# Reordering the first block of a two-block transformer kernel, and dispatching experts inside the turn

## What is computed

```
x: (1, 256, 1024), all float32
first_block, 2 layers l:
  u, q, k, v, gate = rms_norm(x, norm1[l]) @ w_in[l]      # 1024 | 1536 | 1536 | 1536 | 2048 columns
  pooled = multi-window average pooling of u, minus u, through w_pool[l], times pool_scale[l]
  attn   = 12 heads of attention over 256 tokens, with a relative bias table
  m      = gate_a * (pooled @ w_a[l]) + gate_b * (attn @ w_b[l]);  x = x + m @ w_o[l]
  x      = x + (gelu(conv(a)) * b) @ w_down[l]   with a, b = rms_norm(x, norm2[l]) @ w_up[l]
second_block (one layer, with 256 context tokens and a modulation vector silu(c) @ w_ada + b_ada):
  rms_norm(norm_f(x)), modulated; projections; two recurrent mixers and a windowed attention; w_out
  hierarchical mixture of 32 experts (4 groups of 8, the best 2 of the best group per token),
  each expert: (silu(h @ w_gate) * (h @ w_up)) @ w_down
```

## Time and profile before

| | us |
|---|---|
| median of 3 runs | 1995.33 (1994.34 to 1996.38) |
| the profiled execution | 1991.78 |
| its span | 1990.0 |
| TensorE busy, weight loads busy | 1699.0, 1311.2 |
| VectorE, ScalarE, GpSimd busy | 871.2, 596.9, 115.0 |

### The profile page before, as it was taken

One profiled execution on the slowest core, in us unless ns is written; L12 is line 12 of the kernel. 1 busy time (PEld: TensorE's weight loads), 2 busy tenths in 40 slices (PEclk: granted clock), 3 DMA queues, 4 the chain that ended last, 5 costly groups with the idle time before them and its releaser, 6 DMA issues.

```text
span 1990.0 us, 32401 instructions
## 1 busy us (share of the span) xinstructions
PE 1699.0 (85%) x14363; PEld 1311.2 (66%) x14363; DVE 871.2 (44%) x1202; ACT 596.9 (30%) x761; POOL 115.0 (6%) x103
## 2 busy tenths in 40 slices
PE   6999899999899989999989998696987866556665
PEld 6999898998699989899847554385865322112221
DVE  3445566664443556666423744775724111001111
ACT  4344445543334444555321021324213010000000
POOL 0500000000050000000022410000000000000000
PEclk9999999999899999999999998798998998889888
DMA  8651365754675136596434110000069999999998
GB/s 281 230 180 64 127 228 215 271 207 155 234 259 190 64 128 228 213 334 221 148 59 140 43 43 11 1 3 2 3 243 351 373 409 410 410 410 409 410 410 326
DMA packets 154958, 419.94 MB, mean 211 GB/s; under 512 B 14050, under 2 KB 20893, under 8 KB 151762
## 3 DMA queue, kind: packets, MB, share of 16 engines
q1 hardware_dynamic: 154402, 417.87, 56.7%
q10 hardware_dynamic: 432, 0.22, 0.0%
HBM read 416.18 MB, written 1.89 MB: 210 GB/s over the span
## 4 chain that ended last, share of the span: by engine, by line
PE 63%; DMA 19%; DVE 10%; ACT 5%; issue 3%; DVEq 0%; SPq 0%; ACTq 0%
PE bank L1182 29%; DMA R<-w_exp_down 8%; DMA R<-w_exp_up 7%; PE ps_s L1292 3%; PE ps_t L1292 3%; PE bank L1370 3%; PE ps_s L1345 3%; PE bank L1345 2%; ACT w_high L1782 2%; DVE w_low L2187 2%; PE bank L1737 2%; DMA wring<-w_up 2%; PE bank L1722 1%; PE ps_t L1352 1%; DMA wring<-w_in 1%
## 5 line engine op out<-in xcount | busy, mean ns | idle before, releaser
L2187 DVE TENSOR_TENSOR w_low<-wring,w_high 128x2048 fp32r<-128x2048 f32 (+1 forms) x128 | 289.1, 2258 | 329.0 <-ACT w_high L1782 328.4
L1782 ACT ACTIVATE w_high<-wring 128x2048 fp32r<-128x2048 f32 (+1 forms) x128 | 238.2, 1861 | 355.8 <-PE bank L1182 300.0
L1182 PE MATMUL bank<-x_high,w_high 128*128 128x256 f32 x1600 | 325.9, 285 | 18.3 <-DVEq L2215 11.5
L1182 PE MATMUL bank<-x_low,w_high 128*128 128x256 f32 x1600 | 321.5, 283 | 0.0
L1182 PE MATMUL bank<-x_high,w_low 128*128 128x256 f32 x1600 | 319.7, 281 | 0.0
L1182 PEld LDWEIGHTS bank<-x_high,w_high 128*128 128x128 f32 x1600 | 247.4, 191 | 26.0 <-DVEq L2215 12.6
L1182 PEld LDWEIGHTS bank<-x_high,w_low 128*128 128x128 f32 x1600 | 247.8, 190 | 0.0
L1182 PEld LDWEIGHTS bank<-x_low,w_high 128*128 128x128 f32 x1600 | 246.8, 190 | 0.0
L1737 PE MATMUL bank<-R 128*32 128x512 f32 x640 | 94.8, 727 | 63.7 <-DMA R<-w_exp_up 47.9
L1737 PEld LDWEIGHTS bank<-R 128*32 128x32 f32 x640 | 19.9, 124 | 128.6 <-DMA R<-w_exp_up 68.5
L2842 DVE TENSOR_TENSOR R<-bank,R 128x512 f32<-128x512 f32 x8 | 5.5, 693 | 202.3 <-PE bank L1737 202.3
(11 more groups left out here) (584 smaller groups left out, 2688.8 us busy)
## 6 DMA issues: line engine op xcount, KB each, us to landing
wring<-w_in SPq DMA_DIRECT2D x37, 2048.0 KB, 8.0
R<-w_exp_up SPq DMA_DIRECT2D x24, 2048.0 KB, 23.8
R<-w_exp_down SPq DMA_DIRECT2D x24, 2048.0 KB, 23.8
wring<-w_up SPq DMA_DIRECT2D x22, 2048.0 KB, 9.0
R<-w_exp_gate SPq DMA_DIRECT2D x16, 2048.0 KB, 23.4
wring<-w_exp_gate SPq DMA_DIRECT2D x16, 2048.0 KB, 23.7
wring<-w_ada SPq DMA_DIRECT2D x12, 2048.0 KB, 10.8
wring<-w_down SPq DMA_DIRECT2D x10, 2048.0 KB, 7.8
```

What stands on the lines that cost most here:

```text
L1182: mm = pe.matmul(b[:, i * S:(i + 1) * S], left, right, start=k == 0 and m == 0 and i == 0, stop=k == last and m == 2, skip_group_check=True)
L1782: a.activation(high_of(l, job), half_block(l, job, wring), ACT.Copy).then_inc(w_high_ready, 1)
L2187: v.tensor_tensor(half_block(l, job, w_low), half_block(l, job, wring), high_of(l, job).bitcast(F32), ALU.subtract).then_inc(w_low_ready, 1)
```

## The change

- *Start*: the gain row is loaded to one partition by ScalarE's queue, ahead of `ident`; TensorE spreads it by two matmuls with a row of ones into `ps_t`; VectorE multiplies h by it before the norm is known. 1/rms becomes a diagonal matrix (`by_rms`), and layer 0's four `x1` jobs are matmuls with it in place of transposes. The first block comes in two DMAs of four row tiles; high and low parts of its first job are made in halves, the first between `x1` 1 and 2. An operation of the square root function stands ahead of the squares.
- *Order of blocks*: `ada` 4 ahead of `down` 5; `u` 0 of layer 1 ahead of `ada` 5.
- *Gate stage*: the wait for `v` 5 moves into the first `pv`; VectorE takes logits 0 before the low part of gate 1, and the reciprocal is a step of its own behind it; high and low part that belonged to gate 7 (`wa` 1) move behind the pools; the last turned probabilities are copied behind pool 1.
- *wb*: high and low part of `wo` 1 move behind the last split of m.
- *Hand-over*: product and squares in quarters behind each `down` add; two more sums; VectorE's evacuation of the context moves behind the scaling.
- *Experts*: `dispatch` for the next turn moves into the turn, behind `hid`; the columns behind the last expert repeat the first four, and the one behind the loop goes; TensorE waits for the turn's predecessor's last sum before it transposes `put`.

```diff
         if l:
-            ahead.update({("u", 0): (4, 5), ("q", 1): (6,), ("q", 2): (7,)})
+            ahead.update({("q", 1): (6,), ("q", 2): (7,)})
+        else:
+            ahead.update({("down", 5): (4,)})
         for name, j, _ in LAYER_BLOCKS:
             blocks += [(l, "ada", i) for i in ahead.get((name, j), ())]
+            if (l, name, j) == (1, "u", 1):
+                blocks.append((0, "ada", 5))
...
+                if n == 0:
+                    sp.dma_start(dst[:, 0:4, :], src[:, 0:4, :]).then_inc(first_in, 16)
+                    dst, src = dst[:, 4:8, :], src[:, 4:8, :]
                 sp.dma_start(dst, src).then_inc(loaded[n % SLOTS], 16)
...
+                        if l == 0 and name == "x1":
+                            mm = pe.matmul(b[:, kk * P:(kk + 1) * P], xn[:, t, k * P:(k + 1) * P], by_rms[:, t, :],
+                                           start=True, stop=True)
+                        else:
+                            mm = pe.transpose(b[:, kk * P:(kk + 1) * P], xn[:, t, k * P:(k + 1) * P], ident[:, :])
...
+                    halves_first = (l, name, j) == (0, "u", 0)
+                    if halves_first:
+                        pe.wait_ge(first_low, 1)
+                    else:
+                        wait_low(pe, l, (name, j))
                     high, low = high_of(l, (name, j)), half_block(l, (name, j), w_low)
                     last = k_tiles(name) - 1
                     for k in range(last + 1):
+                        if halves_first and k == 4:
+                            wait_low(pe, l, (name, j))
...
                     pe.wait_ge(probT_ready, l * 8 + 2 * hh + 2)
+                    if hh == 0:
+                        wait_emptied(pe, l, ("v", 5))
...
+                if l == 0:
+                    pe.wait_ge(ones_set, 1)
+                    pe.wait_ge(gain_in, 16)
+                    for half in range(2):
+                        mm = pe.matmul(ps_t[:, half * 512:(half + 1) * 512], ones_row, grow[0:1, half * 512:(half + 1) * 512],
+                                       start=True, stop=True)
+                    mm.then_inc(gain_full, 1)
                 if l:
                     wait_emptied(pe, l - 1, ("down", 0))
                     for i in (4, 5):
-                        modulate(l, i)
+                        modulate(l - 1, i)
...
-                wait_emptied(pe, l, ("v", 5))
...
+                pe.wait_ge(y_done, turn(sw_, pair, odd, 4, 4))
...
+            a.dma_start(grow[0:1, :], bass.AP(tensor=d["norm1"].tensor, offset=0, ap=[[0, 1], [1, D]])).then_inc(gain_in, 16)
             a.dma_start(ident[:, :], d["c_ident"]).then_inc(ident_in, 16)
...
+            def first_part(k):
+
+                c = slice(4 * k, 4 * k + 4)
+                if k == 0:
+                    a.wait_ge(first_in, 16)
+                else:
+                    wait_block(a, 0, "u", 0)
+                a.activation(high_of(0, ("u", 0))[:, c, :], half_block(0, ("u", 0), wring)[:, c, :], ACT.Copy)\
+                    .then_inc((first_high, w_high_ready)[k], 1)
+
             def turned(l, name, n):
                 for j in range(4):
+                    if (l, name, j) == (0, "x1", 2):
+                        first_part(0)
...
+                    a.activation(stats[:, 30:31], stats[:, 31:32], ACT.Sqrt)
                     for t in range(ST):
                         a.wait_ge(h_in[t], 16)
-                        a.activation(xn[:, t, :], h[:, t, :], ACT.Square, accum_out=stats[:, t:t + 1]).then_inc(sumsq, 1)
+                        a.activation(squares[:, t, :], h[:, t, :], ACT.Square, accum_out=stats[:, t:t + 1]).then_inc(sumsq, 1)
...
-                    high(l, SPLIT[("gate", i)] + 2)
+                    if i < 7:
+                        high(l, SPLIT[("gate", i)] + 2)
...
+                high(l, SPLIT[("gate", 7)] + 2)
                 pv_high(3)
...
+                    if j < 3:
+                        high(l, SPLIT[("wb", j)] + 2)
                     a.wait_ge(m_ready, 4 * l + j + 1)
                     a.activation(x_high[:, 2 * j:2 * j + 2, :], mT[:, 2 * j:2 * j + 2, :], ACT.Copy).then_inc(m_high_ready, 1)
+                high(l, SPLIT[("wb", 3)] + 2)
...
-            for t in range(ST):
-                wait_emptied(a, DEPTH - 1, ("down", 2 * t + 1))
-                a.activation(junk2, h[:, t, :], ACT.Square, accum_out=st[:, t:t + 1]).then_inc(sumsq2, 1)
-                a.wait_ge(sumsq2, 2 * t + 3)
-                a.wait_ge(hn_ready, t + 1)
-                a.activation(junk2, xs[:, t, :], ACT.Square, accum_out=st[:, 2 + t:3 + t]).then_inc(sumsq2, 1)
-                a.wait_ge(sumsq2, 2 * t + 4)
+            for j in range(4):
+                t, c = j // 2, slice((j % 2) * 512, (j % 2 + 1) * 512)
+                wait_emptied(a, DEPTH - 1, ("down", j))
+                a.activation(junk2[:, 0:512], h[:, t, c], ACT.Square, accum_out=st[:, j:j + 1]).then_inc(sumsq2, 1)
+                a.wait_ge(hn_ready, j + 1)
+                a.activation(junk2[:, 512:1024], xs[:, t, c], ACT.Square, accum_out=st[:, 48 + j:49 + j]).then_inc(sumsq2, 1)
+                a.wait_ge(sumsq2, 2 * j + 4)
...
+                if m == 0:
+                    v.wait_ge(ident_in, 16)
+                    for t in range(ST):
+                        v.tensor_scalar(by_rms[:, t, :], ident[:, :], stats[:, 14 + t:15 + t], None, ALU.mult)\
+                            .then_inc(xs_ready, 1 if t == 0 else 3)
+                    return
...
+                if l == 0:
+                    v.wait_ge(gain_full, 1)
+                    for t in range(ST):
+                        v.wait_ge(h_in[t], 16)
+                        for half in range(2):
+                            c = slice(half * 512, (half + 1) * 512)
+                            v.tensor_tensor(xn[:, t, c], h[:, t, c], ps_t[:, c], ALU.mult)
                 norm(l, 0)
+                turned(l, "x1", 0)
                 if l == 0:
-                    low(l, 0)
-                turned(l, "x1", 0)
+                    first_part(1)
...
-                for i in range(len(SPLIT_IN)):
+                for i in range(len(SPLIT_IN) - 1):
...
+                def row_sums(i):
+                    o = 16 + 3 * (i % 2)
                     v.wait_ge(exp_done, l * 8 + i + 1)
                     v.reciprocal(stats[:, o + 2:o + 3], stats[:, o + 1:o + 2]).then_inc(rsum_ready, 1)
+
+                logits(0)
...
+                low(l, len(SPLIT_IN) + 1)
                 for i in range(8):
-                    logits(i)
+                    if i:
+                        logits(i)
+                    row_sums(i)
                     if i:
                         take_probT(i - 1)
-                    low(l, SPLIT[("gate", i)] + 2)
+                    if i < 7:
+                        low(l, SPLIT[("gate", i)] + 2)
...
-                take_probT(7)
+                    if g == 1:
+                        take_probT(7)
+                low(l, SPLIT[("gate", 7)] + 2)
                 pv_low(3)
...
-                    low(l, SPLIT[("wb", j)] + 2)
+                    if j < 3:
+                        low(l, SPLIT[("wb", j)] + 2)
                     if j:
                         m_low(j - 1)
                 m_low(3)
+                low(l, SPLIT[("wb", 3)] + 2)
...
+                    if l == DEPTH - 1:
+                        c = slice(half * 512, (half + 1) * 512)
+                        wait_emptied(v, l, ("down", j))
+                        v.tensor_tensor(xs[:, t, c], hv, normf[:, c], ALU.mult).then_inc(hn_ready, 1)
...
+            v.wait_ge(sumsq2, 10)
+            chain(v.tensor_tensor(st[:, 52:54], st[:, 0:4:2], st[:, 1:4:2], ALU.add))
+            chain(v.tensor_tensor(st[:, 54:56], st[:, 48:52:2], st[:, 49:52:2], ALU.add))
+            chain(v.tensor_scalar(st[:, 16:18], st[:, 52:54], 1.0 / D, EPS, ALU.mult, ALU.add))
+            chain(v.tensor_scalar(st[:, 18:20], st[:, 54:56], 1.0 / D, None, ALU.mult))
...
-            x2_evac("xc", lambda k: hT[:, k, S:T2], lambda k: mulT[:, 1, k:k + 1], lambda k: mod_col(1, 0, k))
             v.wait_ge(rms2, 2)
             chain(v.reciprocal(st[:, 24:28], st[:, 20:24]))
             for t in range(ST):
                 v.tensor_scalar(xs[:, t, :], xs[:, t, :], st[:, 26 + t:27 + t], None, ALU.mult).then_inc(xs2_ready, 1)
+            x2_evac("xc", lambda k: hT[:, k, S:T2], lambda k: mulT[:, 1, k:k + 1], lambda k: mod_col(1, 0, k))
...
+            chain(v.tensor_copy(comb[:, :, N_EXP:], comb[:, :, 0:QUAD]))
+            chain(v.tensor_scalar(posm[:, :, N_EXP:], posm[:, :, 0:QUAD], -float(SLOTS_E), None, ALU.add))
...
+                chain.base = sw_ * per_sweep + pair * (2 * DISPATCH_CHAIN) + (second + odd * DISPATCH_CHAIN)
+                chain.n = 0
+                dispatch(bass.ds(pair * (2 * QUAD) + (odd + 1) * QUAD, QUAD))
...
-                        chain.base = sw_ * per_sweep + pair * (2 * DISPATCH_CHAIN) + (second + odd * DISPATCH_CHAIN)
```

(7 more changed lines are left out.)

40 lines of the change are left out of this document (23 added, 17 removed).

## The result

The changed kernel takes 1960.88 us (median of 4 runs, 1957.3 to 1967.21) against 1995.36 us before (4 runs, 1994.34 to 1996.38). The ratio is 0.9825, 95% interval 0.9807 to 0.9844. Forecast were 1954.2 us, range 1946 to 1966. The profiled execution took 1963.2 us, its span is 1961.4.

The account below looks back on a forecast made before the run. The expert loop was taken as bound by its weight stream, so only its start could move, by shortening the chain before it. Terms summed to 41.1 us: 1950.7 us profiled, 1954.2 us on the median's scale, range 1946 to 1966.

Parts of the forecast that it names:

- Start: Layer 0's start up to `u` job 0: 3.6 us earlier plus half of 2.35 us slow clock, 4.9 us (3.6 to 6.0).
- Rival 3: Start: diagonal matmuls slower than transposes; if four times slower, 11 us lost, 1965 us; chance 0.02.
- Gate stage: Per layer: front 4.0 us (2.5 to 4.1) and tail 5.7 us (3.0 to 6.2) from removed or shorter TensorE waits.
- Layer boundary: Between the layers: adds no longer queue behind u's split, TensorE's 7.3 us wait goes; 9.4 us (5.5 to 10.6).
- Rival 2: Layer boundary: block 5 lands late and becomes the wait; at 10.8 us it costs 3 us, 1957 us; chance 0.10.
- Rival 4: Layer boundary: halves or order do not bite, adds still queue behind the split; gives 1 us, 1963 us; chance 0.09.
- Rivals 5 and 6: Expert loop: 5, added wait runs the ring dry, slower, 2002 us, chance 0.01; 6, not stream-bound, 1942 us, chance 0.03.
- wo: Per layer: the 1.7 us wait in `wo` 0 goes, `wo` 1 waits about 1 us; 1.1 us (0 to 1.7).
- Hand-over: Second block's start: less VectorE work behind the last add, transposes and projection earlier; 4.3 us (3.0 to 5.0).
- Experts: Expert loop: −0.4 us ahead of the first dispatch, nothing from dispatch inside the turn, +1.3 us at the end.
- Rival 1: TensorE's clock falls anyway behind the shorter idles before `u` and pv 3, some at the hand-over: 1960 us; chance 0.18.
- The page on the table load: Gate stage: with about 2.66 us per table switch, not 1.28, exp comes 1.4 us later; sum 38.5 us.

Follow-up runs that it names:

- gain_dma: The changed kernel with the gain row spread over 128 partitions by DMA, and transposes of the scaled product in place of diagonal matmuls: 1954.05 us, ratio 0.9801.
- gate_front: The changed kernel with the front of the gate stage undone (wait for `v` 5 ahead of gate 0, low part of gate 1 before logits 0): 1969.17 us, ratio 0.9855.
- block_order: The changed kernel with the order of blocks alone undone (`ada` 4 and 5 behind `down` 5, ahead of `u` 0): 1970.11 us, ratio 0.9867.
- best: gain_dma plus idle TensorE transposes ahead of `u` 0 and `up` 0, at the hand-over and ahead of each turn's down blocks: 1953.26 us, ratio 0.9785.

## Why the prediction was right, and where its sum was off

*Direction and mechanism*: right. Four stalls of TensorE went, the 1 us at pv 3 and `wo` 1 that was forecast took part of their place, and the stream of the experts started 31 us earlier (the prediction had some 40) at the same rate. The time fell into the range, 6.7 us above the point. The sign "a DMA wait appears in a layer where there was none" came in part: ScalarE had waited for `up` blocks before too, but the wait that this hands to TensorE grew, in `up` of layer 0 from at most 1.0 to 2.17 us and at the second norm of layer 1 from 0.46 to 1.69. Both have no term in the sum.

*Start*, forecast 4.9, was 1.1. The mis-sized terms are "Two slow matmuls of 512 columns (estimate 0.86 each ...)", which measured 3.78 us for 1.7, and the diagonal jobs, taken at a transpose's price, which measured 5.79 for 3.65. The four instructions of the gain spread start at 6.25, 7.27, 8.12 and 8.97 us: 0.86 was about the price of one instruction, and only the count was wrong. Rival 3 had this mechanism, at 2%, with "for it speaks no row". A row did: line 1722's matmuls stand in the earlier trace rows as x256, where the code has 128 (8 turns of 16), while the transposes of line 1213 stand as x96 for 96. At 275 ns for each instruction such a matmul costs twice a transpose. I had compared the mean of one instruction and not counted the instructions. The 5.79 us are 1.6 times the 3.65 and not twice because the clock turned full at 17.63 us, in the midst of them. The third part of the miss is the pace of TensorE: "of the 2.35 us of slow clock half may go" came true, and more than that, in the nine profiles with the long diagonal jobs; gain_dma has the forecast's chain and no full pace until 22.34 us.

*Gate stage*, forecast 9.7 a layer, was 9.9 and 9.9, by gate_front 4.1 for the front. *Layer boundary*, forecast 9.4, was 10.1, of which 8.6 by the order and 1.5 by a fall of the clock at `u` 0 that the kernel before had in its profile and the changed one had not; the prediction had left open which it would be. Against block_order, without that difference, it was 9.6. Rival 2, block 5 late, did not come: the modulation matmuls ran without a wait. Rival 4 neither; block_order shows the adds behind the split when the order is undone. Rivals 5 and 6 did not come: the stream stands at 409 to 410 GB/s before and after.

*wo*, forecast 1.1 a layer, was 0.8 and −0.6. In layer 1 the second norm's transposes waited 1.69 us (0.46 before): the last `wo` add had queued behind a low part whose weight block had landed late. That part of the loss, and the late block in `up` of layer 0 (with the half clock behind it between nothing and 1.6 us against the kernel before, by profile), goes with a 2 MB block that lands late for a job that now comes sooner. What sets the landing was not tried.

*Hand-over*, forecast 4.3, is 5.2 to 5.5 by the start of the projection, 3.0 where the clock fell behind it. *Experts*: the end is worth 1.1 (forecast 1.3), the dispatch inside the turn nothing else, as said. *Tail*: no term in the forecast. The half clock there costs 1.2 to 2.9 us, in eight of eleven profiles of changed kernels without idle transposes in the turn. The kernel before has one profile, with none of it at the last block, but with half clock at other blocks in the same turn (1964.08: 1.94 us for 8 matmuls, 1.07 at full); that the change brought this loss isn't shown.

*Rival 1*, the clock falls anyway, priced at 1960, is nearest to what happened, though not where I had put it: pv 3 never fell behind its 1.05 us (2.86 us for its 12 matmuls in the change), while the three waits of 1.8 us, which I had taken from one profile as harmless ("the one in layer 0 slowed nothing"), fell in 16 of 29 cases. That 1960 lies so close to the 1960.88 is luck: it was summed from places where the clock held. One execution can't price a matter of chance.

*The page on the table load*: the row keeps 1.28 us, as before, now at 1.71 us of the span, under the wait for x, and the gate loop's gain of 9.9 a layer leaves no room for the 1.4 us that the Trainium skill's figure (ScalarE: Activation LUTs, What ACT_TABLE_LOAD costs) would have taken from it. In the kernel before, ScalarE is idle for 0.02 us ahead of the load at 8.35 us and 0.01 behind it, so no drain shows.

## What to carry to other kernels

Before you price an operation by the mean of its rows, divide their count by the count in the code: that is where a matmul of two instructions shows. Where the wait of an engine with a changing clock is shortened to about 2 us, price the restart as a chance and not as a fact, and take it from several profiles; idle transposes in the wait held the clock up in all nine cases at `u` 0 and `up` 0 here, though no gain of theirs is told apart in the times. When a stall is removed, look first at whether the adds that release everyone queue behind a bulk operation with slack: moving that one paid 9 to 10 of the 28.6 us between the two profiles here.

## What the runs showed of the hardware

- **A plain float32 matmul is two instructions, a transpose one**: 32 against 16 for the same 16 tiles, each 0.213 us behind the one before at half clock (in the change and in gain_dma) and 0.11 at full, so twice the time at one clock. The 5.79 us against 3.67 are less than twice, since the clock turned full on the way. The Trainium skill (TensorE: Matmul & The Clock Gate, Terms) calls the transpose mode four times faster for FP32; these traces show twice.
- **A clock fall at a restart of this kernel costs 1.5 us or nothing** (one case of 16 cost 1.06), behind a wait of 1.8 us, in about every second case: in two executions of one program at none of three places and at all three. The Trainium skill (same page, Part 1) says that the number of slow matmuls at a kernel's start differs from run to run; the traces agree: in these two executions the clock turned full 11.4 and 12.5 us after TensorE's first matmul.
- **Transposes can bring TensorE to full pace**: in the kernel before it had run nothing but 16 of them (from 10.98 to 14.63 us) when the granted clock turned full at 14.83, and in best it turned full at 14.84, behind the same 16 and in the midst of the 12 idle ones, so that `u` 0 runs at 20 matmuls per 2 us. It isn't certain: in gain_dma the same 16 left it to turn full at 22.34. The same page (Part 4: PE-mode transpose) says that the full clock doesn't engage for the transpose mode, since it isn't counted as the engine's work. Here the runs decide: it can.
- **At the head of a program a granted clock of 1.00 can mean that there is no record**: 11 matmuls in 2 us in gain_dma from 18 to 22 us, 20 in best, both rows with 1.00. gain_dma's trace has its first record at 22.34 us, best's at 14.84; the kernel before, whose records begin at 14.83, reads 0.50 from 20 to 22 us. Up to the first record the count of matmuls per window tells the pace, the view does not.
